# Work moved between the heads of two mixers, and the last normalisation cut in parts, in a three-layer transformer kernel

## The reference, cut to what matters

```python
h = _rmsnorm(x, norm_mix_g)
c_q, c_kv, k_r, x_m, z, i_pre, f_pre = _split_in(h @ w_in)
q  = _rmsnorm(c_q, q_norm_g) @ w_uq;  kv = _rmsnorm(c_kv, kv_norm_g) @ w_ukv
attn_out = _mla_attention(...)                       # 8 heads, chunk mask, softmax
xc = silu(_causal_conv(x_m, conv_w, conv_b))
mq, mk, mv = xc @ w_mq, xc @ w_mk * ML_HD ** -0.5, x_m @ w_mv
hm = _mlstm_chunkwise(mq, mk, mv, ig, fg)            # 4 heads, done here as decayed attention
hm = (hm - mean) * rsqrt(var + EPS) * mh_norm_g
ml_out = (hm + ml_skip * xc) * silu(z)
x = x + concat([attn_out, ml_out]) @ w_o
x = x + _hier_moe(_rmsnorm(x, norm_ffn_g), ...)      # 2 of 32 experts for each token
hp = _rmsnorm(x, norm_ple_g)
x = x + (p @ w_ple) * sigmoid(hp @ w_ple_gate)
return _rmsnorm(x, final_norm_g)
```

## Time and profile before

| | us |
|---|---|
| median of three runs | 1010.97 |
| the profiled execution | 1011.97 |
| its span, first to last instruction | 1010.40 |
| PE busy | 955.8 |
| DVE busy | 635.3 |
| ACT busy | 534.4 |

### The profile page before, as it was taken

One profiled execution on the slowest core, in us unless ns is written; L12 is line 12 of the kernel. 1 busy time (PEld: TensorE's weight loads), 2 busy tenths in 40 slices (PEclk: granted clock), 3 DMA queues, 4 the chain that ended last, 5 costly groups with the idle time before them and its releaser, 6 DMA issues.

```text
span 1010.4 us, 14997 instructions
## 1 busy us (share of the span) xinstructions
PE 955.8 (95%) x5635; PEld 733.8 (73%) x5635; DVE 635.3 (63%) x1392; ACT 534.4 (53%) x973; POOL 84.1 (8%) x97
## 2 busy tenths in 40 slices
PE   6999899999999999999999999999899999987796
PEld 5777588888888877688888888867676665443355
DVE  4679768999945566768999945667876221110046
ACT  5757667676634565767666644765742211100054
POOL 0100001122100302001122101010000000000000
PEclk9999999999999999999999999999899999999998
DMA  8934246655565544246655664414577999999971
GB/s 272 384 131 126 91 125 200 202 177 180 200 204 173 203 146 146 84 138 197 204 171 188 199 184 142 149 48 167 209 305 306 396 419 420 421 420 421 421 280 44
DMA packets 99359, 224.58 MB, mean 222 GB/s; under 512 B 9535, under 2 KB 64210, under 8 KB 86994
## 3 DMA queue, kind: packets, MB, share of 16 engines
q1 hardware_dynamic: 99122, 223.04, 61.8%
q10 hardware_dynamic: 160, 0.53, 0.2%
HBM read 222.50 MB, written 1.05 MB: 221 GB/s over the span
## 4 chain that ended last, share of the span: by engine, by line
PE 76%; DMA 10%; DVE 8%; ACT 3%; SPq 2%; issue 1%; DVEq 0%; ACTq 0%
PE ps L559 72%; DMA ringx<-in_w_up_e_dram 6%; PE ps L563 3%; DMA ring<-in_w_up_e_dram 3%; DVE wl L1991 2%; DVE smb L2005 1%; DMA ring<-in_w_uv_dram 1%; SPq L2993 1%; SPq L2996 1%; DMA ring<-in_w_in_even_dram 1%; ACT L1443 1%; ACT wh L1446 0%; DVE pb L1996 0%; ACT hh L1443 0%; DVE x L1991 0%
## 5 line engine op out<-in xcount | busy, mean ns | idle before, releaser
L1991 DVE TENSOR_TENSOR wl<-ring,wh 128x1024 fp32r<-128x1024 f32 (+3 forms) x212 | 268.8, 1270 | 106.6 <-ACT wh L1446 105.3
L1446 ACT ACTIVATE wh<-ring 128x1024 fp32r<-128x1024 f32 (+3 forms) x212 | 222.2, 1051 | 105.6 <-PE ps L559 101.3
L559 PE MATMUL ps<-hx,wh 128*128 128x512 f32 (+1 forms) x720 | 245.0, 387 | 0.1
L559 PE MATMUL ps<-hx,wl 128*128 128x256 f32 x704 | 196.6, 280 | 0.0
L559 PEld LDWEIGHTS ps<-hx,wh 128*128 128x128 f32 x720 | 133.7, 187 | 28.8 <-issue 0.6
L559 PEld LDWEIGHTS ps<-hx,wl 128*128 128x128 f32 x704 | 133.1, 189 | 0.0
L559 PE MATMUL ps<-ring,xg 128*32 128x256 f32 (+1 forms) x592 | 79.4, 388 | 7.2 <-DMA ring<-in_w_gate_e_dram 4.2
L2938 POOL TENSOR_TENSOR fs<-fs,rt 128x256 f32<-128x256 f32 x44 | 52.4, 1213 | 357.1 <-ACT fs L1443 357.1
L559 PE MATMUL ps<-wh,hh 128*128 128x512 f32 (+3 forms) x192 | 79.7, 415 | 2.2 <-DVE wl L1991 2.1
L559 PE MATMUL ps<-wl,hh 128*128 128x512 f32 (+3 forms) x192 | 75.1, 391 | 0.0
L559 PE MATMUL ps<-wh,hl 128*128 128x512 f32 (+3 forms) x192 | 73.0, 388 | 0.0
(11 more groups left out here) (317 smaller groups left out, 1674.8 us busy)
## 6 DMA issues: line engine op xcount, KB each, us to landing
ring<-in_w_up_dram SPq DMA_DIRECT2D x88, 512.0 KB, 4.8
ring<-in_w_down_dram SPq DMA_DIRECT2D x22, 1024.0 KB, 5.0
ring<-in_w_up_e_dram SPq DMA_DIRECT2D x19, 1024.0 KB, 18.1
ring<-in_w_gate_e_dram SPq DMA_DIRECT2D x18, 1024.0 KB, 13.7
ring<-in_w_down_e_dram SPq DMA_DIRECT2D x15, 1024.0 KB, 26.0
ringx<-in_w_down_e_dram SPq DMA_DIRECT2D x14, 1024.0 KB, 21.0
ring<-in_w_in_odd_dram SPq DMA_DIRECT2D x12, 1024.0 KB, 5.2
ringx<-in_w_gate_e_dram SPq DMA_DIRECT2D x12, 1024.0 KB, 15.7
```

Source lines behind the costliest of these rows:

```text
L559: return e.matmul(o, l, r, start=start, stop=stop)
L1446: return e.activation(o, i, ACT.Copy)
L1991: return e.tensor_tensor(o, a, b, op)
```

## The change: two orders and the end

**First mixer.** On PE the transposes of `dqT` come before the value product of the last fox heads, and the half chunk of the output projection of step 10 moves behind the first pair of dsa scores, to step 12. On DVE a pair of heads is now served together: both `maxima` stand at the even step, `mix_lo` of fox between the first two, and the split of a weight chunk comes at odd steps. Excerpts of PE's rows ahead of the second pair of scores, before and after (`ptb,big` is the value product, `cst,big` the transposes, `sA` scores, `wh,mh` the output projection):

```diff
@@ tensor: first mixer
                 if i == 10:
                     rotation[:] = [4, 5, 1]
-                    next(outp)
...
+                if i == 12:
+                    next(outp)
                 h = head_at.get(i)
...
                 if i == 9:
                     for _ in side:
                         pass
+                    q.wait_ge(s_rdq, 1)
+                    to_T("dqT", ...)
                 h = 7 if i == 9 else head_at.get(i - 3)
...
-                if i == 9:
-                    q.wait_ge(s_rdq, 1)
-                    to_T("dqT", ...)
@@ scalar: second mixer
-            swish(0)
             for i in (1, 3):
                 evac(flat(qT3[0:96, 2 * i:2 * i + 2, :]), "q2T", i, rows=96)
+            swish(0)
...
                     copy(mix[:, 1, 512:1024], b[:, :]).then_inc(of(drained, "ml", 1), 1)
+                    for m in range(4):
+                        emptied(q, "z", m)
+                    act(szT[:, :, :], szT[:, :, :], ACT.Silu).then_inc(s_sz, 1)
+                if i == 12:
+                    next(outp)
+                if i == 13:
+                    warm()
+                    mix_hi("mla", 1, mla_hi[:, 1, :])
+                    q.wait_ge(s_var, RV["mln"])
+                    act(st[:, 16:24], st[:, 8:16], ACT.Sqrt).then_inc(s_std, 1)
                     q.wait_ge(s_xc, 2)
                     for h in range(4):
                         act(xcT[:, h, :], xcT[:, h, :], ACT.Copy, scale=gain("sk2", h))
-                if i == 12:
-                    ...  (the SiLU of z, warm)
-                if i == 13:
-                    ...  (the square root)
-                if i in out_at[2]:
-                    next(outp)
...
+                if i in (13, 14):
+                    next(outp)
+            next(outp)
-            mix_hi("mla", 1, mla_hi[:, 1, :])
@@ scalar: tail
-                for t, n in ((0, 0), (1, 0), (0, 1)):
-                    sigmoid(t, n)
+                sigmoid(0, 0)
+                sigmoid(1, 0)
+                q.wait_ge(s_sgm, 1)
+                act(xs[:, 0, 0:512], x[:, 0, 0:512], ACT.Square, accum_out=st[:, 3:4]).then_inc(s_sqh, 1)
+                sigmoid(0, 1)
                 q.wait_ge(s_sgm, 3)
-                act(xs[:, 0, :], x[:, 0, :], ACT.Square, accum_out=st[:, 0:1]).then_inc(s_sq, 1)
+                act(xs[:, 0, 512:1024], x[:, 0, 512:1024], ACT.Square, accum_out=st[:, 0:1]).then_inc(s_sq, 1)
+                act(st[:, 63:64], cst[:, C_ONE:C_ONE + 1], ACT.Sqrt)
                 root("fin0", 1)
                 act(st[:, 61:62], cst[:, C_ONE:C_ONE + 1], ACT.Sigmoid)
-                sigmoid(1, 1)
+                sigmoid(1, 1, 2)
                 warm()
                 root("fin1", 1)
+                q.wait_ge(s_rstd, RV["fin1"])
+                act(xs[:, 1, 0:512], sg[:, 1, 0:512], ACT.Copy, scale=st[:, 25:26]).then_inc(s_xna, 1)
@@ vector: first mixer
-                    mix_lo("fox", 1, bank_of(mh1, 1), bank_of(ml1, 1), 2)
...
+                if h is not None and h >= 8 and h % 2 == 0:
+                    maxima(h, h, dsam, 0.125, smb1)
+                    if h == 8:
+                        mix_lo("fox", 1, bank_of(mh1, 1), bank_of(ml1, 1), 2)
+                    maxima(h + 1, h + 1, dsam, 0.125, smb1)
@@ vector: second mixer
-            split_lo(c_in2[0] + 6, wh, wl)
...
             next(side)
+            split_lo(c_in2[0] + 6, wh, wl)
...
+                if i == 11:
+                    next(hms)
+                if i == 2:
+                    next(proj)
+                    next(proj)
...
+                if i == 12:
                     next(hms)
-                if i in (12, 13):
+                if i == 13:
+                    mix_lo("mla", 1, mla_hi[:, 1, :], mla_lo[:, 1, :], 10)
                     next(hms)
-                if i == 14:
-                    mix_lo("mla", 1, mla_hi[:, 1, :], mla_lo[:, 1, :], 10)
                 if i == 0:
-                    next(proj)
-                    next(proj)
                     gate_rows(0)
@@ vector: tail
+                gated(0, 0, 512, 1)
+                gated(1, 0, 512, 2)
                 half(0)
+                own.inc(ts(st[:, 4:5], st[:, 1:2], 1.0 / DM, EPS, ALU.mult, ALU.add))
+                gated(0, 512, 1024, 3)
+                own.inc(tt(sg[:, 1, 0:512], x[:, 1, 0:512], gfl[:, 0:512], ALU.mult))
...
+                second_root("fin0", st[:, 0:1], st[:, 5:6], st[:, 24:25])
+                stt(xs[:, 0, :], x[:, 0, :], st[:, 24:25], gfl[:, :], ALU.mult, ALU.mult).then_inc(s_xn, 1)
+                gated(1, 512, 768, 4)
+                gated(1, 768, 1024, 5)
                 half(1)
+                second_root("fin1", st[:, 2:3], st[:, 4:5], st[:, 25:26])
+                stt(xs[:, 1, 512:1024], ..., st[:, 25:26], gfl[:, 512:1024], ALU.mult, ALU.mult).then_inc(s_xn, 1)
```

More of the change, by code:

```diff
@@ L971, in tensor @@
                         pass
+                    q.wait_ge(s_rdq, 1)
+                    to_T("dqT", [lambda t, g=g: prj[:, t, 1544 + g * P:1544 + (g + 1) * P] for g in range(4)])
                 h = 7 if i == 9 else head_at.get(i - 3)
@@ L986, in tensor @@
                     next(side, None)
-                if i == 9:
-                    q.wait_ge(s_rdq, 1)
-                    to_T("dqT", [lambda t, g=g: prj[:, t, 1544 + g * P:1544 + (g + 1) * P] for g in range(4)])
             rotation[:] = [4, 5, 6, 7]
@@ L2310, in vector @@
                 if i == 10:
-                    mix_lo("fox", 1, bank_of(mh1, 1), bank_of(ml1, 1), 2)
                     q.wait_ge(s_mask, 1)
                 h = head_at.get(i)
-                if h is not None:
-                    maxima(h, h, MA if h < 8 else dsam, 0.125, smb1)
+                if h is not None and h < 8:
+                    maxima(h, h, MA, 0.125, smb1)
                 h = head_at.get(i - 1)
@@ L2334, in vector @@
                     next(proj, None)
[L2335 to L2338, removed]
+                if i < 10:
+                    for _ in range(out_at[0].count(i - 1)):
+                        next(outp)
+                elif i % 2:
+                    for _ in range(out_at[0].count(i - 1) + out_at[0].count(i - 2)):
+                        next(outp)
+                elif i == 20:
+                    for _ in range(out_at[0].count(i - 1)):
                         next(outp)
@@ L2872, in tail, with gated @@
                 rinv("np2", 2, DM, rin[:, 14:16])
[L2874 to L2879, removed]
+                def gated(t, c0, c1, upto):
+                    q.wait_ge(s_sg, upto)
+                    own.inc(tt(sg[:, t, c0:c1], sg[:, t, c0:c1], ple[:, t, c0:c1], ALU.mult))
+                    tt(x[:, t, c0:c1], x[:, t, c0:c1], sg[:, t, c0:c1], ALU.add).then_inc(s_sgm, 1)
@@ L2891, in tail @@
                 q.wait_ge(s_gf, 16)
-                for t, n in ((0, 0), (1, 0), (0, 1)):
-                    gated(t, n)
+                for t, n in product(range(2), range(2)):
+                    emptied(q, "ple", t, n)
+                gated(0, 0, 512, 1)
+                gated(1, 0, 512, 2)
                 half(0)
+                own.inc(ts(st[:, 4:5], st[:, 1:2], 1.0 / DM, EPS, ALU.mult, ALU.add))
+                gated(0, 512, 1024, 3)
+                own.inc(tt(sg[:, 1, 0:512], x[:, 1, 0:512], gfl[:, 0:512], ALU.mult))
@@ L2895, in tail @@
+                q.wait_ge(s_sqh, 1)
+                own.inc(ts(st[:, 5:6], st[:, 3:4], 1.0 / DM, EPS, ALU.mult, ALU.add))
                 q.wait_ge(s_sq, SQ["fin0"])
-                rinv("fin0", 1, DM, st[:, 24:25])
-                last(0, 0, DM)
-                gated(1, 1)
+                second_root("fin0", st[:, 0:1], st[:, 5:6], st[:, 24:25])
+                stt(xs[:, 0, :], x[:, 0, :], st[:, 24:25], gfl[:, :], ALU.mult, ALU.mult).then_inc(s_xn, 1)
+                gated(1, 512, 768, 4)
@@ L2899, in tail @@
+                gated(1, 768, 1024, 5)
                 half(1)
-                own.inc(tt(st[:, 0:1], st[:, 1:2], st[:, 2:3], ALU.add))
-                rinv("fin1", 1, DM, st[:, 25:26])
-                for n in range(2):
-                    last(1, n, 512)
+                second_root("fin1", st[:, 2:3], st[:, 4:5], st[:, 25:26])
+                stt(xs[:, 1, 512:1024], x[:, 1, 512:1024], st[:, 25:26], gfl[:, 512:1024], ALU.mult, ALU.mult).then_inc(s_xn, 1)
             either(e, "DVE", q, own, tail)
@@ L3005, in sync @@
             od = out[0].rearrange("(t p) d -> p t d", p=P)
-            for i, (t, n, width) in enumerate(((0, 0, DM), (1, 0, 512), (1, 512, 512))):
-                q.wait_ge(s_xn, 3 + i)
+            for t, n, width, done, upto in ((0, 0, DM, s_xn, 3), (1, 0, 512, s_xna, 1), (1, 512, 512, s_xn, 4)):
+                q.wait_ge(done, upto)
                 e.dma_start(od[:, t, n:n + width], xs[:, t, n:n + width]).then_inc(s_out, 16)
```

29 lines of the change are left out of this document (14 added, 15 removed).

## The result

The changed kernel is slower: 1012.89 us (median of 20 runs, 1011.21 to 1015.86) against 1011.05 (20 runs, 1009.78 to 1012.54), a ratio of 1.0021 with an interval of 1.0015 to 1.0028. I had forecast 1003.6, and a range up to 1008.4. The profiled execution is one of the long ones, 1014.99 us with a span of 1013.1, so it is 2.1 us above its median, as before's was 0.9 above its own.

A forecast was written before the change was run, and what follows sets the result against it. PE's work and waits were taken to bound the kernel outside the MoE. Terms 3.5 + 0.7 + 1.5 + 1.6 + 0.1 = 7.4 us gave 1003.6 against the median of 1010.97, with a range of 1000.8 to 1008.4.

The forecast's parts named there:

- the first of the second mixer: Second mixer's start: the split moved behind the sums of squares removes the c_q wait, 0.7 us gained, bounds 0 and 0.8.
- rival 1: DVE gives back more, PE's saved rests becoming waits for DVE: only 2.8 us gained, 1008.2; chance 0.17.
- rival 4: Slower: the clock falls on many small waits at three places, 9.0 us lost against 7.4 gained, 1012.6; chance 0.05.
- The first mixer: First mixer: reordering cuts PE's waits and DVE sets the pace, 3.5 us gained, bounds 1.5 and 4.9.
- `next(proj)`: Second mixer, early steps: moving the split that waited for ACT removes z and `maxima` waits, 1.5 us, bounds 0.5 and 2.1.
- The second mixer's end: End of second mixer: `ptb` wait and half clock go, most given back; 1.6 us gained, bounds −1.6 and 3.5.
- From the mixers to the end: MoE stretch: its stream starts as much earlier as PE and DVE do, so the gain passes on in full.
- rival 3: MoE: the expert weight stream holds its own time, so the second mixer's gain is lost; 3.6 us gained, 1007.4; chance 0.08.
- The kernel's end: Kernel's end: last output leaves at 1007.3 and not 1007.4, 0.1 us gained, between a loss of 0.6 and gain of 0.7.
- The lower bound: Whole kernel: sum of the parts' low bounds, 1.5 + 0 + 0.5 + 0.8 and nothing at the end, 2.8 us, 1008.2.

The follow-up runs named there:

- experiments 3 and 5 to 7: The kernel before with one part alone: the moved split 1016.87 us, the first mixer's part 1009.22, the kernel's end 1010.96, the second mixer's end 1010.98.
- the mended end: Changed kernel with the split put back and ACT's and DVE's splits, scalings and products reordered at the second mixer's end: 1008.51 us, ratio 0.9974.
- experiments 8 and 9: Kernel before with next(proj) moved to step 2: 1007.32 us; with the first mixer's part too: 1006.66; these plus second mixer's end 1007.42, or kernel's end 1006.62.
- experiments 7 and 10: Kernel before with the second mixer's end alone: 1010.98 us; changed kernel with the split put back and that end reordered on ACT and DVE: 1008.51.

## Why the prediction was wrong

- **The step that failed is the first of the second mixer.** I wrote that the chunk of the moved split "is needed by PE at 645.7 and is ready at 645.5", and valued the move at a gain of 0.7, bounds 0 and 0.8. The chunk was the one that PE took up at 641.30; 645.7 belongs to the next one, whose first product started at 646.52 before. DVE did have c_q ready 0.8 us earlier (its scalings start at 641.38, and at 642.15 with the split put back), but nothing was gained by it: PE, held by the missing chunk, came to c_q only at 648.33. What the move brought was a 4.1 us wait and a stretch at half clock: 4.0 and 5.1 us lost in the two jobs in which the changed kernel ran beside the one with the split put back, 6.3 with the split alone. Since my bound ended at 0, the range had no room for it. This is neither rival 1 (DVE gives back more) nor rival 4 (many small waits): it is one large wait at the one place where I had priced a move without finding the first reader of what it makes. It is not the only step: with the split put back the kernel measured 1009.09 and 1008.42, a gain of 1.4 and 2.6 us and not of 7.4; the first lies outside my range too, the second at its edge.
- **The first mixer** got 2.2 us shorter against the profile before and 1.7 against those without its clock fall, not 3.5, and alone gave 1.3 us. I had added up DVE's work and put the last transposes of `pb` at 125.1; they came at 126.89, in a profile that was 0.5 us late before them. I had left PE 0.9 us of waits; 3.3 were there between 108 and 125 us. What the sum over DVE left out is that PE also waits for banks: with two `maxima` behind two `normed`, transposes wait until the maxima have drained a bank, 1.7 us of the 3.3. The 1.65 us of slow clock in my upper bound was too much too: that fall cost 0.5 us.

```profile
112.65 0.52 PE L563 MATMUL ps<-cst,pb 128*128 128x128 f32 x3 [0.76 <-DVE mxb L2015]
...
117.66 0.52 PE L563 MATMUL ps<-cst,pb 128*128 128x128 f32 x3 [0.97 <-DVE mxb L2015]
```

- **`next(proj)`**, my 1.5 us (bounds 0.5 and 2.1), was right in its waits and too small in time: 3.7 us. From the transposes of c_q to the end of the mixer PE took 94.6 to 97.5 us in the five profiles with the old place (before and experiments 3 and 5 to 7) and 92.8 to 93.3 in those with the new one (the mended end apart, 94.2). 1.8 us of it is between the one old profile at full clock throughout and a new one, and that is the size of my term. Part of the rest goes with the clock: in three of the five profiles with the old place it was at half somewhere from 684 to 695 us, behind the waits for z and `maxima`, in none of the 13 with the new one. By 97.45 us with such a fall and 96.18 without, it cost 1.3 us. I did not trace what remains.
- **The second mixer's end** is worth about 0 and not 1.6. I had every new wait within 0.4 us (1.05 for `wl` where I said 1.1, 1.62 for `mh` where I said 2.0). The error is in what they replace: the same stretch took as long with the old order wherever the clock had not fallen. From the transposes of c_q to the mixer's end it was 92.84 and 92.85 us with the old end (experiments 8 and 9) and 92.88 to 92.97 with the new one. In the profile with `next(proj)` alone, the 2.9 us wait and the 6 us behind it:

```profile
715.06:717.95 2.89, 0.01 (x1) 0.03 (x1) 2.43 (x10) 2.86 (x6) 0.00 (x0) 1.00 0.03 11
717.95:723.95 6.00, 5.39 (x27) 4.01 (x28) 4.60 (x10) 5.47 (x11) 0.00 (x0) 1.00 0.68 239
```

  I had booked the 6.00 us at 0.50 in the earlier trace rows as a consequence of the wait, with certainty, at 3.0 us. Of eight profiles with this wait five fell to half clock there and three did not, and the fall cost less than half its length: 0.4 us when it was 3.4 us long (93.22 and 93.27 against 92.84), 1.6 when it was 6.8 (96.18 against 94.60).
- **From the mixers to the end** the shift is passed on, as forecast (rival 3 falls): with the split put back the mixer ended 4.9 us earlier than before (736.47), the span 4.6. Over all 18 profiles, the ten in which the mixer ended early (736.9 us in the mean) reached the first `gated` at 990.0, the eight others (742.1) at 994.8. What varies in between is the router's clock (11.1, 12.8 or 14.5 us for none, 3.4 or 6.8 us at half) and the stretch behind it, 238.7 to 241.8 us long; the latter I have not traced.
- **The kernel's end** was forecast at 0.1 and measured at 0, within 1.1 us: right as far as that tells.
- **The lower bound** was also summed up wrongly. I had bounded the second mixer's end by a loss of 1.6 us, but rival 1 takes it as a gain of 0.8. With my own bound the sum is 0.4 us, 1010.6, and the range should have gone as far. It would still not have held 1012.89.
- **Rival 4** came true in part, though not in the three profiles of the changed kernel: behind the new waits of 1.6 and 1.7 us at the second mixer's end the clock fell in two of the ten profiles that have that end (experiments 7 and 10).
- **What stays open.** Alone the parts give -1.3, -3.7, 0, 0 and +6.3, together +1.3 us; the changed kernel measured +1.8, +2.6 and +2.5. The difference of about 1 us is within what the intervals allow (that of the split alone is 1.9 us either way), and I have not traced it.

The version that beats both kernels is the first mixer's part and the two moved calls: 0.9968 and 0.9961 in two jobs, by the medians 4.2 and 4.1 us below the kernel before and 6.6 below the changed one in the last job.

## What to carry to other kernels

Before a step is moved behind something else, find the first instruction that reads what it makes, by its start in the timeline of the reading engine, and take the gap between the two as the slack; a reader that starts right when the writer ends, with no wait shown, has none. Half clock seen behind a wait in one profile is a chance and not a price: a second profile, or the spread of the runs, tells which. And where two engines feed a third through a stretch, add up their work there before reordering it: if the sum is the stretch, the order only chooses where the third one waits.

## What the runs showed of the hardware

- **Stretches at half clock** were 3.4 or 6.8 us long in all 18 profiles, as long as PE had work, at full clock before and behind. What one costs depends on who sets the pace. In the router, which took 11.1, 12.8 or 14.5 us, it cost 1.7 or 3.4. In the first mixer the stretch of 111 to 114 us is missing in three profiles of the old order there, and the mixer was only 0.5 us shorter for it (59.6 against 60.1 us): in its place PE waited 0.9 us more for `pb` (4.0 in all and not 3.1).
- **What stood before them**: the wait of 4.1 us in four of four profiles (once with 6.8 us of half clock), that of 2.9 us for `ptb` in five of eight; that of 2.3 us not, in the one profile that had it. Shorter ones did it too: 1.0 and 1.1 us for z and `maxima` in three of five, 1.6 or 1.7 at the new end of the second mixer in two of ten. In the MoE, where PE waits for the loads of weights from about 870 us on, five profiles fell behind such a wait, of 2.9 us in three and of 2.0 and 1.9 in one each, while waits of 2.0 and 1.9 in two others brought none. So the length of the wait alone does not tell. The Trainium skill, "TensorE: Matmul & The Clock Gate", Part 1, says of the slow matmuls at a kernel's start that the same kernel shows a different count of them from one run to the next. What the traces show is the like in the middle of a kernel: three profiles of the changed kernel had half clock in the router for 6.8, 3.4 and 0 us.
- **A busy PE can fall too.** In 13 of the 18 profiles the clock fell between 740 and 753 us though PE is shown busy but for 0.4 us. What runs there are 16 transposes and then 32 products of 36 columns, in which the weight loads are busy nearly as long as the products, and the fall came 2.2 to 4.0 us behind the first of these; in the profile with the split put back a second time:

```profile
736.90:741.00 4.10, 3.69 (x33) 3.44 (x31) 3.81 (x9) 3.49 (x8) 0.00 (x0) 1.00 1.03 434
741.00:748.00 7.00, 7.00 (x23) 4.76 (x23) 5.57 (x28) 4.00 (x7) 0.00 (x0) 0.54 0.84 350
```

  The spread of 3 to 6 us among runs of the kernel before is of the size of two or three such stretches; that they are its whole cause was not tested.
